# Second feature pass in units of 256 and 288 columns with packed rows, and seven weight forms at seven distances from the token rows

## What is computed

```python
def trunk_layer(x, c, w_ada, b_ada, w_in, conv_w, ...):
    shift, scale, gate = jnp.split((jax.nn.silu(c) @ w_ada + b_ada)[:, None, :], 3, axis=-1)
    h = x * (1 + scale) + shift
    proj = h @ w_in
    qa = proj[..., COL_QA:COL_KA].reshape(head_shape)
    ...
    qkv, new_conv = short_conv(proj[..., COL_QKVB:COL_ZB], conv_buf, conv_w)
    ...
    merged = jax.nn.sigmoid(proj[..., COL_GA:COL_GB]) * branch_a + jax.nn.sigmoid(proj[..., COL_GB:]) * branch_b
    out = merged @ w_o
    x_new = layer_norm(DEEPNORM_ALPHA * x + gate * out, ln_g, ln_b)
```

## Time and profile before

| | |
|---|---|
| median of 3 runs | 2371.31 us (2370.66 to 2374.88) |
| the profiled execution | 2376.29 us |
| its span | 2374.5 us |
| mean granted clock of TensorE | 0.976 |
| TensorE busy | 2260.8 us, 95% |
| VectorE busy | 1631.9 us, 69% |
| ScalarE busy | 1169.0 us, 49% |
| GpSimd busy | 374.4 us, 16% |

### The profile page before, as it was taken

How to read it: one execution, slowest core, us unless ns; L and a number is a source line. 1 busy time by engine, 2 the same in 40 slices (tenths; PEclk the granted TensorE clock), 3 DMA queues, 4 the chain that set the end, 5 groups by cost and what they waited for, 6 DMA issues and landing times. The chain is left out here.

```text
span 2374.5 us, 45041 instructions
## 1 busy us (share of the span) xinstructions
PE 2260.8 (95%) x16842; PEld 2028.3 (85%) x16842; DVE 1631.9 (69%) x4008; ACT 1169.0 (49%) x2457; POOL 374.4 (16%) x627
## 2 busy tenths in 40 slices
PE   5999999999999999999999989979998899999998
PEld 2778788888899999999999978658887689999786
DVE  5877776554363676776655558668986877778797
ACT  4444444444431554444444468647776533333554
POOL 0010100000111111110000001123321035445100
PEclk8999999999999999999999999979999699999999
DMA  7232323333532233223333367975565656666663
GB/s 272 98 116 98 116 98 116 107 107 96 203 103 77 92 110 115 92 98 112 112 110 95 109 257 233 343 220 163 149 179 183 197 174 212 195 205 232 197 210 124
DMA packets 256970, 363.56 MB, mean 153 GB/s; under 512 B 55655, under 2 KB 191439, under 8 KB 252273
## 3 DMA queue, kind: packets, MB, share of 16 engines
q1 hardware_dynamic: 197408, 224.24, 30.6%
q0 software_dynamic: 36496, 124.94, 13.7%
q10 hardware_dynamic: 22848, 11.50, 1.8%
HBM read 246.94 MB, written 113.68 MB: 152 GB/s over the span
## 5 line engine op out<-in xcount | busy, mean ns | idle before, releaser
L328 PE MATMUL ps_f<-m_lo,w_hi 128*128 128x272 f32 (+1 forms) x2436 | 787.8, 323 | 12.4 <-DVE m_lo L656 5.6
L328 PE MATMUL ps_f<-m_hi,w_lo 128*128 128x272 f32 (+1 forms) x2436 | 785.9, 323 | 0.0
L328 PE MATMUL ps_f<-m_hi,w_hi 128*128 128x272 f32 (+1 forms) x2436 | 784.5, 322 | 0.0
L328 PEld LDWEIGHTS ps_f<-m_lo,w_hi 128*128 128x128 f32 x2436 | 459.4, 189 | 52.7 <-issue 16.4
L328 PEld LDWEIGHTS ps_f<-m_hi,w_hi 128*128 128x128 f32 x2436 | 458.7, 188 | 32.2
L328 PEld LDWEIGHTS ps_f<-m_hi,w_lo 128*128 128x128 f32 x2436 | 459.2, 189 | 31.6
L720 DVE TENSOR_TENSOR stage<-partial,ps_f 128x512 f32<-128x512 f32 (+2 forms) x348 | 183.5, 544 | 303.6 <-PE ps_f L328 293.8
L461 ACT ACTIVATE partial<-ps_f 128x272 f32<-128x272 f32 (+1 forms) x348 | 161.1, 463 | 369.7 <-PE ps_f L328 368.7
L423 ACT ACTIVATE w_hi<-w_raw 128x512 fp32r<-128x512 f32 x348 | 213.0, 626 | 190.3 <-PE ps_f L328 110.6
L627 DVE TENSOR_TENSOR w_lo<-w_raw,w_hi 128x512 fp32r<-128x512 f32 x348 | 239.1, 688 | 83.0 <-ACT w_hi L423 79.0
L746 DVE SCALAR_TENSOR_TENSOR conv<-stage,side,conv 128x1024 f32<-128x1024 f32 x108 | 138.3, 1281 | 8.2 <-ACT conv L477 6.9
(11 more groups left out here) (772 smaller groups left out, 4686.9 us busy)
## 6 DMA issues: line engine op xcount, KB each, us to landing
w_raw<-in_w_feat SPq DMA_DIRECT2D x58, 1024.0 KB, 5.8
gates<-scratch_g_d SPq DMA_DIRECT2D x56, 256.0 KB, 3.3
m_rows<-scratch_parts_d SPq DMA_DIRECT2D x16, 768.0 KB, 4.7
z_f<-scratch_z_d ACTq DMA_DIRECT2D x13, 768.0 KB, 6.7
scratch_conv_d<-conv POOLq DMA_DIRECT2D x18, 544.0 KB, 3.0
scratch_conv_d<-conv POOLq DMA_DIRECT2D x18, 512.0 KB, 2.9
kc<-in_k_cache SPq DMA_DIRECT2D x8, 1152.0 KB, 12.0
vc<-in_v_cache POOLq DMA_DIRECT2D x8, 1152.0 KB, 11.1
```

The lines of the kernel that those rows point to most:

```text
L328: last = pe.matmul(out[:, 0:n], l[:, cols], r, start=start and k == 0 and nth == 0, stop=k == KH - 1 and nth == 2, skip_group_check=not start)
```

## The change

- `CUT` becomes 256: unit 0 has 256 columns, all of the prompt, unit 1 has 288, 256 of the prompt and the 32 of the samples.
- The token tiles of the second pass are laid out by unit (`of_unit`): first four packed rows of 256, then four packed rows of 288. Loads, modulation, samples, the gathering of the samples' tokens and the reading of the token rows in the value stage follow. A load is three transfers in place of two, a modulation eight activations of 256 columns in place of four of 512.
- The fourteen weight tiles become slices of one tile `w_forms`, in which form j starts `FORMS_AT[j]` elements later than before: 0, 8, 24, 32, 40, 48, 56 elements, 0 to 224 bytes. This holds in both passes.
- `S_BANK`, the place of the samples' norms in a bank, moves from column 272 to 288. `AHEAD_0` is 0 and changes nothing.

```diff
-CUT = (HT + SS) // 2
+CUT = HT // 2
 WIDE = HT + SS
-UNITS = (((0, HT),), ((0, CUT), (CUT, CUT)))
+UNITS = (((0, HT),), ((0, CUT), (CUT, HT + SS - CUT)))
...
+AHEAD_0 = 0
+FORMS_AT = (0, 8, 24, 32, 40, 48, 56)
...
-            wh, wl = [], []
-            for j in range(7):
-                wh.append(sb(f"w_hi{j}", [P, KH * P], F32R, early))
-                wl.append(sb(f"w_lo{j}", [P, KH * P], F32R, early))
+            w_forms = sb("w_forms", [P, 14 * KH * P + FORMS_AT[6]], F32R, early)
+            form_at = lambda j, low: (2 * j + low) * KH * P + FORMS_AT[j]
+            wh, wl = ([w_forms[:, form_at(j, low):form_at(j, low) + KH * P] for j in range(7)] for low in range(2))
...
-        S_BANK = D_BANK[0:2 * SUB, CUT:CUT + SAMP]
+        S_BANK = D_BANK[0:2 * SUB, WIDE - CUT:WIDE - CUT + SAMP]
...
+        def of_unit(x, u):
+
+            at, n = UNITS[1][u]
+            return x.rearrange("p k n -> p (k n)")[:, KH * at:KH * (at + n)].rearrange("p (k n) -> p k n", n=n)
...
-                sp.dma_start(dst[:, :, 0:HT], t["x_T"][:, k:k + KH, at:at + HT]).then_inc(x_in[s, m], 16)
-                if s:
-                    sp.dma_start(dst[:, :, HT:], t["x_T"][:, k:k + KH, SEQ + SS * h:SEQ + SS * (h + 1)]).then_inc(x_in[s, m], 16)
+                if s == 0:
+                    sp.dma_start(dst[:, :, 0:HT], t["x_T"][:, k:k + KH, at:at + HT]).then_inc(x_in[s, m], 16)
+                    return
+                for u in range(2):
+                    sp.dma_start(of_unit(dst, u)[:, :, 0:CUT], t["x_T"][:, k:k + KH, at + CUT * u:at + CUT * (u + 1)]).then_inc(x_in[s, m], 16)
+                sp.dma_start(of_unit(dst, 1)[:, :, CUT:], t["x_T"][:, k:k + KH, SEQ + SS * h:SEQ + SS * (h + 1)]).then_inc(x_in[s, m], 16)
...
-                    hi, lo = tokens(m_hi[x], s)[:, k, at:at + n], tokens(m_lo[x], s)[:, k, at:at + n]
+                    hi, lo = ((of_unit(y[x], u) if s else tokens(y[x], s))[:, k, :] for y in (m_hi, m_lo))
...
-                        hi, lo = (tokens(y[slot(*key)], s)[:, k % KH, at:at + P] for y in (m_hi, m_lo))
+                        rows_of = (lambda y: of_unit(y, at // CUT)[:, k % KH, at % CUT:at % CUT + P]) if s else (lambda y: tokens(y, 0)[:, k % KH, at:at + P])
+                        hi, lo = (rows_of(y[slot(*key)]) for y in (m_hi, m_lo))
...
-                act.wait_ge(x_in[key], 16 * (1 + s))
+                act.wait_ge(x_in[key], 16 * (1 + 2 * s))
...
-                    last = act.activation(x[:, k, 0:HT], x[:, k, 0:HT], ACT.Identity, scale=mods[:, KT + n, 0:1], bias=mods[:, n, 0:1])
+                    for part in ([of_unit(x, u)[:, k, 0:CUT] for u in range(2)] if s else [x[:, k, 0:HT]]):
+                        last = act.activation(part, part, ACT.Identity, scale=mods[:, KT + n, 0:1], bias=mods[:, n, 0:1])
```

More of the change, by code:

```diff
@@ L120, in modulate_and_project @@
         with ExitStack() as early:
-            sb("w_place", [P, 4 * KT * P + TO_TILES + 7 * KH * P], where=early)
+            sb("w_place", [P, 4 * KT * P + TO_TILES + 7 * KH * P + FORMS_AT[3]], where=early)
             w_sum = sb("w_sum", [P, KH * P], where=early)
@@ L134, in modulate_and_project @@
             vl.append(sb(f"wv_lo{j}", [P, KT, VW], F32R))
-        sb("w_rest", [P, 4 * KT * P + TO_TILES + 14 * KH * P - 5 * KT * VW])
+        sb("w_rest", [P, 4 * KT * P + TO_TILES + FORMS_AT[6] + 14 * KH * P - 5 * KT * VW])
         with ExitStack() as early:
@@ L208, in tokens @@
                 return x[:, :, :]
-            return x.rearrange("p k n -> p (k n)")[:, 0:KH * HT].rearrange("p (k n) -> p k n", n=HT)
+            return x.rearrange("p k n -> p (k n)")[:, AHEAD_0:AHEAD_0 + KH * HT].rearrange("p (k n) -> p k n", n=HT)
+        def of_unit(x, u):
+            at, n = UNITS[1][u]
+            return x.rearrange("p k n -> p (k n)")[:, KH * at:KH * (at + n)].rearrange("p (k n) -> p k n", n=n)
         def slot(s, m):
@@ L668, in samples @@
                 h, k0 = int(m[0]) - 1, KH * (int(m[1]) - 1)
-                dve.wait_ge(x_in[1, m], 32)
-                xx = x[:, :, HT:].rearrange("p k (s e) -> p k s e", e=TS)
+                dve.wait_ge(x_in[1, m], 48)
+                xx = of_unit(x, 1)[:, :, CUT:].rearrange("p k (s e) -> p k s e", e=TS)
                 part = lambda f0: bc(mods[:, f0 + k0:f0 + k0 + KH, 1 + HS * h:1 + HS * (h + 1)], TS)
@@ L775, in gather @@
                 for dst, src in ((e_hi, m_hi[i]), (e_lo, m_lo[i])):
-                    put(dve.tensor_copy(dst[:, k0:k0 + KH, SS * h:SS * (h + 1)], f32(src[:, :, HT:])), e_put)
+                    put(dve.tensor_copy(dst[:, k0:k0 + KH, SS * h:SS * (h + 1)], f32(of_unit(src, 1)[:, :, CUT:])), e_put)
             def take_values(v):
```

## The result

The changed kernel takes 2387.76 us (median of 4 runs, 2383.0 to 2390.51) against 2371.31 us before: a ratio of **1.0062**, 95% interval 1.005 to 1.0074. It is 0.6% slower, where 2363.1 us was forecast, and lies outside the range of 2346 to 2377. The profiled execution took 2389.44 us, its span is 2387.7 us, 13.2 more than before.

A forecast was written before the change was run, and what follows sets the result against it. TensorE's matmul starts were taken to bound the second pass; -9.5 us there, 0 in the first pass and +1.3 in the value stage sum to -8.2, so 2371.3 becomes 2363.1 us, range 2346 to 2377.

The forecast's parts named there:

- What bounds the kernel: Second pass: it lasts as long as its matmuls take from start to start; what a matmul saves, the end saves.
- The first pass, distances: First pass, 512 columns on shifted weight forms: taken as 0, bounds 16.6 us gained and 8.8 us lost.
- The rule of the Trainium skill: Both passes: gap N/2.4 + 2.5 ns and independent read ports, so new widths gain nothing and distances do nothing; not followed.
- The second pass, width: the 288 columns: Second pass, unit 1: 132.3 ns per matmul, taken between 272 and 320 columns; bounds 127.5 and 133.4.
- I let one quarter take the slow step: Second pass, unit 0: 256 columns at 114.4 ns, from 113.3 and 117.5; with 288 columns, 9.5 us gained.
- Who must keep up: Second pass: ScalarE and VectorE keep pace with the shorter unit 0 and longer unit 1; costed at nothing.
- The value stage: Modulation of the fourth tile, eight activations for four, delays TensorE: 1.3 us lost, between 0 and 1.3.
- The distances cost in the first pass: Rival, chance 0.17: 2088 matmuls of 512 columns on shifted forms cost 8.8 us; 2382 us in all.
- Widths and distances even out: Rival, chance 0.21: 256 columns stay slow or steps are streaming plus a constant; pass -0.7 to +1.5 us, 2371 to 2374.

The follow-up runs named there:

- E2: The kernel before with only the seven weight distances added, units still 272 columns: 2387.75 us, ratio 1.0064.
- E1: The changed kernel with all seven weight forms at distance 0, new widths and packed rows kept: 2379.58 us, ratio 1.003 to the kernel before.
- constant runs: The changed kernel with all seven forms at one distance: 192, 64 or 32 bytes; ratios 1.0021, 1.0065 and 1.0066 to the kernel before.
- H1: The changed kernel with form 6 at 192 bytes like form 5, in place of 224: 2387.45 us in one execution.
- I1: F2 with one extra matmul of 64 columns ahead of each unit 0 of the second pass: 2364.64 us in one execution; timed again, ratio 0.9957.
- F2: The changed kernel with all forms at 64 bytes and the first pass's token rows moved by 64 bytes too, so its distance is 0: 2374.12 us, ratio 1.0007.
- I4: F2 with one extra matmul of 256 columns ahead of each unit 0 of the second pass: 2372.48 us in one execution.
- K2: I1, extra matmul of 64 columns kept, with all forms at distance 0 in both passes: 2379.74 us in one execution.
- G1: The changed kernel with form 0 at 160 bytes, forms 1 to 6 at 192, first pass's token rows moved by 192: 2376.72 us, ratio 1.0014.
- F1: The changed kernel with all seven forms at 64 bytes: 2389.08 us, ratio 1.0065 to the kernel before.
- F4: F2 with the second pass's rows 544 elements apart as before, not packed: 2371.99 us, ratio 0.9997 to the kernel before.
- E4: The changed kernel with all seven forms at 192 bytes: 2377.03 us, ratio 1.0021 to the kernel before.

## Why the prediction was wrong

**Two terms of the sum failed; the others held.** Forecast, for the second pass, the first pass and the value stage: -9.5, 0 and +1.3 us. Measured: -0.3, +11.6 and +1.0.

- *What bounds the kernel.* Right. The end moved with the starts of the matmuls: the differences of the two passes and the value stage make 12.3 of the span's 13.2 us, with no new wait in the second pass.
- *The first pass, distances: "I take 0."* This is the step that made the change slower. It measured +11.6 us, shown by E2, which has only this, and by E1, which lacks it and has the first pass of before. The sum's upper bound of 8.8 us was too low as well: I had taken the 4.2 ns between two steps at 256 columns as the price of a shifted form at 512; measured, the six shifted forms pay 232.6 - 226.8 = 5.8 ns each on average (6.5 at 32 bytes, 2.1 at 192 in the constant runs). The reasoning failed where it took "two steps exist at one and the same distance" to mean "that distance sets little". At 256 columns both hold: the distance sets which steps there are (120.0 at 0; 113.3 or 117.8 at 64), and what stands ahead goes with which of them it is. That 226.7 ns hold over places that differ by multiples of 512 bytes is no row on the others at all, and I used it as one.
- *The rule of the Trainium skill* (TensorE: Matmul & The Clock Gate, Step-by-step: what each phase is for), that two independent read ports keep the weight load from the running matmul, would make the distances do nothing. E2 measured otherwise: the same loads and the same matmuls, other places, 5 ns more per matmul. What in the memory does it isn't shown by that; that the distance does something is. The gap of the same page (Back-to-back issue gap), which the page gives for a single matmul and not for a stream in which each has its load of weights, would give the new widths together what the old ones took. The pass came out 0.3 us shorter, but of steps (118.1 and 132.6 ns) that the gap gives for neither.
- *The second pass, width: the 288 columns.* Right, 132.6 ns against 132.3.
- *The second pass, width: "I let one quarter take the slow step."* This is the step that took the gain away. The 256 columns took 118.1 ns, not 114.4; 3.7 ns x 2436 = 9.0 us, nearly the whole 9.5. My range ended at 117.5, and five of the seven forms lie above it (118.1 to 119.7): it had not the third step, that of distance 0, in it, since no row of the trace shows a stream of 256 columns at 0. The rows stand at 64 bytes, where none of the seven forms lies, and those of the earlier trace rows are not packed either: `u1_hi` has rows of 320 columns, of which these matmuls read 256. I carried a step from one distance to seven others. And of the two steps of the earlier trace rows the good one is no share of chance within a run: undisturbed, a run of products keeps its step (H1, and all 84 matmuls of unit 0 in I1); behind a wait or the norm matmuls it can change (F2, I4). The same rows, weights and distance gave 117.8 in F2 and 113.3 in I1, with one matmul of 64 columns ahead.
- *Who must keep up.* Right, at nothing: TensorE's waits in the pass are those of before, 1.7 and 0.7 us.
- *The value stage.* The sum came near (+1.0 for +1.3), in part by luck. The modulation of the fourth tile takes 4.05 us where the earlier trace rows had 2.95:

```profile
690.95 4.05 ACT L450 ACTIVATE m_sum<-m_sum,ada_mods 128x256 f32<-128x256 f32 x8 [15.55 <-DMA m_sum<-in_x_T]
...
705.52 0.36 PE L66 MATMUL ps_f<-wv_lo,m_hi 128*128 128x268 f32 x1 [0.74 <-DVE v_rows L797]
```

  But TensorE's wait behind it, 0.87 us in the earlier trace rows, is 0.74 and not 2.2. The tile's load reached ScalarE sooner: 6.3 us from its issue at 684.62 us to the modulation, 7.6 in the kernel before (issued at 670.95). That time is 6.2 us in K2, 7.2 in E1 and 7.8 in G1, whose transfers and modulations are those of the changed kernel, and the wait follows it: 0.6, 1.6 and 1.9 us, against 0.87 at 7.6 us before. So the longer modulation does reach TensorE, by about the 1.1 us that it is longer, and a quicker load hid it in the profiled execution of the changed kernel. The microsecond came from elsewhere, from the clock. Behind the 3.7 us in which TensorE waits for `wv_lo`, in both kernels, the granted clock falls to 0.50, 1.2 GHz, and the matmuls start 222 ns apart: 15 of them before, 23 in the changed kernel (columns as in the earlier trace rows; first the kernel before).

```profile
612.80:616.30 3.50, 3.50 (x18) 3.50 (x18) 0.04 (x1) 2.54 (x2) 0.00 (x0) 0.51 0.97 328
...
624.70:629.40 4.70, 4.70 (x23) 4.70 (x23) 0.00 (x0) 3.40 (x4) 0.00 (x0) 0.50 0.97 336
```

  Eight more at 0.10 us each over the usual 119 ns are 0.8 of the 1.0 us. Their number goes from none in F1 to 29 in F4 and G1, so I don't put it down to the change.

**The rivals.** "The distances cost in the first pass" is what happened, with its place right and its price too small: 2382 us was said, 2387.8 measured. At once the second pass went as in "Widths and distances even out", which the 2382 had in it. I gave this rival 0.17, because every row of the first pass shows one distance; that is a reason for a wide bound, not for a low chance.

**What stays open.** Why a certain matmul ahead leads into one step or the other: at 64 bytes a narrower one (64, 128, 192 columns) gave the good one from the second product on at the latest, in all 29 pairs; one of 256 columns, or the 288 columns of unit 1 straight ahead, gave the bad one in most pairs. A wait ahead turned it to the good one in F2 and I4 and not in E4, and the norm matmuls turned it one way in G1 and I4 and the other way in the changed kernel and H1. That the extra matmul works by its width, and not by the time at which the matmuls behind it start, was not told apart. At 192 bytes no extra matmul was tried. What in the memory makes some distances slower wasn't told apart either; 96, 128, 160 and 224 bytes were measured only with jumps. The stretch between the passes is 2.5 us longer than before in F2 and F4 and 3.3 in G1. In each, 1.0 us of this is the longer wait, and 10, 14 and 14 more matmuls at 1.2 GHz are 1.0, 1.4 and 1.4 us; the rest stays open.

## What to carry to other kernels

Where TensorE's stream sets the end and waits are gone, the place of the weights against the moving rows, modulo 256 bytes, is a parameter like the width. Here it was worth up to 6.5 ns of 227 at 512 columns and up to 6.7 of 120 at 256. It has to be measured for each width, since 512 columns were fastest at 0 and 256 at 64 or 192. Where a step is carried over from another stretch, its distance has to be carried over with it, counted in the same direction. A stretch that shows one place only says nothing of another, so a change that moves tiles in a stretch with no gain to make there should leave that stretch as it was. A steady step read at one spot of a trace can be one of two, and a single narrow matmul at the start of a run may pick the better, as it did at 64 bytes.

## What the runs showed of the hardware

- With rounded fp32 and 128 weight columns loaded per matmul, the step of 512 columns went from 226.8 ns to 228.9 at 192 bytes and 233.3 at 32 and 64 bytes between weights and rows.
- 256 columns in packed rows took 113.3, 117.8 or 120.0 ns in a steady stream, and 118.3 at 32 bytes; 120.0 is that of distance 0. At 64 bytes the same 84 matmuls took either of the others, and an extra matmul of 64 columns in front, 29 in all, made the pass 7.5 us shorter (618.7 to 611.2 us).
- 288 columns hardly care: 132.2 to 133.3 ns. 272 columns, whose rows lie at 0 and 128 bytes in unit 0 and at 64 and 192 in unit 1 when the forms are at 0, took the same on average over the seven distances of the forms (E2, 620.9 and 620.6 us).
- Behind a wait of 3.7 us TensorE's granted clock fell to 0.50 or 0.51 for 15 matmuls in one kernel and 23 in another, which then started 222 ns apart in place of some 119.
